# Three rounded products for the experts' down projection, on one Trainium2 core

## What is computed

```python
N_EXPERTS = 64; TOP_K = 8; D_MODEL = 1024; EXPERT_FF = 256; MOE_BLOCK = 128

def swiglu(x, w_gate, w_up, w_down):
    return (jax.nn.silu(x @ w_gate) * (x @ w_up)) @ w_down

def routed_experts(h, top_i, top_w, w_gate, w_up, w_down):
    # assignments sorted by expert, each expert's rows padded to blocks of 128
    ...
    def block(args):
        tok, e = args
        return swiglu(h_pad[tok], w_gate[e], w_up[e], w_down[e])
    out = lax.map(block, (row_tok.reshape(n_blocks, MOE_BLOCK), blk_exp))
    out = out.reshape(n_rows, D) * row_w[:, None]
    return jax.ops.segment_sum(out, row_tok, num_segments=T + 1)[:T]
```

## Time and profile before

| | us |
|---|---|
| median of 3 runs | 2048.01 |
| lowest and highest | 2043.39, 2048.45 |
| the profiled execution | 2049.21 |
| its span, first to last instruction | 2047.6 |
| mean granted TensorE clock | 0.975 of full |

### The profile page before, as it was taken

How to read it: one execution, slowest core, us unless ns; L and a number is a source line. 1 busy time by engine, 2 the same in 40 slices (tenths; PEclk the granted TensorE clock), 3 DMA queues, 4 the chain that set the end, 5 groups by cost and what they waited for, 6 DMA issues and landing times. The chain is left out here.

```text
span 2047.6 us, 34503 instructions
## 1 busy us (share of the span) xinstructions
PE 1928.1 (94%) x10264; PEld 1495.0 (73%) x10265; DVE 1038.1 (51%) x1532; ACT 874.1 (43%) x1210; POOL 373.5 (18%) x337
## 2 busy tenths in 40 slices
PE   4999999899899999989789999999999999999995
PEld 3999999899788666755547777777777777777772
DVE  4113401166438335545426666666666666666665
ACT  5110111244212212221246666666666666666663
POOL 0100100111111000000212222232223222222220
PEclk9999999899899999999889999999999999999997
DMA  7211311111443665425069896999998888897964
GB/s 260 74 52 41 123 52 31 32 63 62 144 142 113 229 230 206 143 85 196 1 228 347 261 346 182 317 295 300 331 301 271 269 273 306 244 352 253 300 180 172
DMA packets 182101, 399.64 MB, mean 195 GB/s; under 512 B 22425, under 2 KB 87185, under 8 KB 182046
## 3 DMA queue, kind: packets, MB, share of 16 engines
q1 hardware_dynamic: 149166, 312.16, 42.5%
q0 software_dynamic: 31680, 82.49, 15.7%
q10 hardware_dynamic: 1200, 4.26, 0.6%
HBM read 351.27 MB, written 80.64 MB: 211 GB/s over the span
## 5 line engine op out<-in xcount | busy, mean ns | idle before, releaser
L2184 DVE TENSOR_TENSOR wexp_lo<-wexp,wexp_hi 128x2048 fp32r<-128x2048 f32 x190 | 426.9, 2288 | 91.3 <-ACT wexp_hi L2135 88.3
L2135 ACT ACTIVATE wexp_hi<-wexp 128x2048 fp32r x190 | 353.4, 1907 | 52.4 <-issue 49.4
L2111 PE MATMUL bank<-wexp_down,hTe 128*128 x736 | 330.6, 592 | 0.0
L2086 PE MATMUL bank<-wexp_hi,x_hi 128*128 128x512 f32 x744 | 300.5, 404 | 3.8 <-DVE wexp_lo L2184 3.8
L2086 PE MATMUL bank<-wexp_hi,x_lo 128*128 128x512 f32 x744 | 292.0, 393 | 0.0
L2086 PE MATMUL bank<-wexp_lo,x_hi 128*128 128x512 f32 x744 | 290.4, 390 | 0.0
L2059 POOL DMA_INDIRECT acc_d<-ob,ixs x92 | 153.7, 1670 | 615.8 <-DMA acc_d<-ob,ixs 441.9
L2111 PEld LDWEIGHTS bank<-wexp_down,hTe 128*128 128x128 f32 x736 | 139.1, 189 | 139.4 <-issue 132.3
L547 PE MATMUL bank<-hT_hi,w_hi 128*128 128x344 f32 x576 | 187.3, 325 | 7.3 <-DVEq L659 7.3
L547 PE MATMUL bank<-hT_hi,w_lo 128*128 128x344 f32 x576 | 185.1, 321 | 0.0
L547 PE MATMUL bank<-hT_lo,w_hi 128*128 128x344 f32 x576 | 184.6, 320 | 0.0
(11 more groups left out here) (357 smaller groups left out, 2988.7 us busy)
## 6 DMA issues: line engine op xcount, KB each, us to landing
wexp<-in_w_exp_gate SPq DMA_DIRECT2D x128, 512.0 KB
wexp<-in_w_exp_up SPq DMA_DIRECT2D x128, 512.0 KB
wexp_down<-in_w_exp_down SPq DMA_DIRECT2D x128, 512.0 KB
wada<-in_w_ada SPq DMA_DIRECT2D x12, 2048.0 KB, 10.9
w_raw<-in_w_in SPq DMA_DIRECT2D x44, 512.0 KB, 3.9
gates_d<-gst POOLq DMA_DIRECT2D x48, 172.0 KB, 2.1
gate<-gates_d SPq DMA_DIRECT2D x16, 516.0 KB, 5.8
xn<-in_x_prompt ACTq DMA_DIRECT2D x8, 512.0 KB, 8.3
```

The lines of the kernel that those rows point to most:

```text
L2086: last = pe.matmul(banks[0][:].rearrange("p (g n) -> p g n", g=2), stat[:, b, k, :], mov[:, b, :, k * FF:(k + 1) * FF], start=(k == 0 and ...
L2111: last = pe.matmul(banks[4 + half][:], hT[:, f, :], wdn[:, bass.ds(slot, 1), f, half * 512:half * 512 + 512].rearrange("p a n -> p (a n)") ...
L2135: act.activation(w_hi[:, b, g, :], wexp[:, bass.ds(e & (RING - 1), 1), g, :].rearrange("p a n -> p (a n)"), ACT.Copy).then_inc(whi_ok, 1)
L2184: dve.tensor_tensor(w_lo[:, b, g, :], wexp[:, bass.ds(e & (RING - 1), 1), g, :].rearrange("p a n -> p (a n)"), w_hi[:, b, g, :], ALU.subtr ...
```

## The change

The down weights are split like the others. ACT rounds each half (`round_down`, `down_hi`), between its two `wexp_hi`; DVE takes the rest (`rest_of_down`, `down_lo`), after the first of its two `wexp_lo`; the second `wexp_lo` moves to the start of the next block, behind a table load of its own. The hidden rows are split in the same way (`turned`: `hTe_hi` by ACT, `hTe_lo` by DVE). PE takes 12 rounded products of 512 columns for the 4 in float32, and transposes the hidden rows of the next block at the end of a block, no longer at its start. The ring of the down weights has 2 slots, no longer 4, and a slot is loaded anew once it has been split. On ACT, `ob` comes after all of the splitting; `hh` takes the place of `sg`. The diff, cut to its core:

```diff
--- before.py
+++ after.py
@@ -455,7 +455,7 @@
             def far(name, shape, dt=F32):
                 return sb(name, shape, dt, c5, "right")
 
-            wdn = far("wexp_down", [P, RING, FF // P, D])
+            wdn = far("wexp_down", [P, 2, FF // P, D])
             wexp = far("wexp", [P, RING, 2, KD * FF])
             table = far("table", [1, ITEMS + AHEAD, 2], I32)
             starts = far("starts", [1, E], I32)
@@ -1909,15 +1909,18 @@
         w_lo = tile("wexp_lo", [P, 2, 2, KD * FF], F32R)
...
         sg = tile("sg", [P, FF])
-        hh = tile("hh", [P, FF])
-        hT = tile("hTe", [P, FF // P, P])
+        hh = sg
+        hT_hi = tile("hTe_hi", [P, FF // P, P], F32R)
+        hT_lo = tile("hTe_lo", [P, FF // P, P], F32R)
+        d_hi = tile("down_hi", [P, 2, FF // P, 512], F32R)
+        d_lo = tile("down_lo", [P, 2, FF // P, 512], F32R)
         ob = tile("ob", [P, 2, D])
         wcol = tile("wcol", [P, RING])
         none = tile("none", [ROW0, D // 4])
         ixs = [tile(f"ixs{b}", [P, 1], U32) for b in range(2)]
-        names = "ix ixs tp xhi xlo wc whi wlo gu sg h hp hT dn ob scat wu wd pad".split()
-        (ix_ok, ixs_ok, x_tp, xhi_ok, xlo_ok, wc_ok, whi_ok, wlo_ok, gu_ps, sg_ok, h_ok, h_tp, hT_ok, dn_ps, ob_ok, added,
-         up_ok, _, pad_ok) = (sem("s6" + n) for n in names)
+        names = "ix ixs tp xhi xlo wc whi wlo gu sg h hp hThi hTlo dhi dlo0 dlo1 dn ob scat wu pad".split()
+        (ix_ok, ixs_ok, x_tp, xhi_ok, xlo_ok, wc_ok, whi_ok, wlo_ok, gu_ps, sg_ok, h_ok, h_tp, hThi_ok, hTlo_ok, dhi_ok,
+         dlo0_ok, dlo1_ok, dn_ps, ob_ok, added, up_ok, pad_ok) = (sem("s6" + n) for n in names)
         passed = sem("s6passed")
         kept_in, ended = sem("s6kept"), sem("s6ended")
 
@@ -1945,6 +1948,10 @@
+        def down_half(e, half):
+            return wdn[:, bass.ds(e & 1, 1), :, 512 * half:512 * half + 512].rearrange("p a f n -> p (a f) n")
@@ -1968,25 +1975,23 @@
 
                 def next_down(part, g):
 
-                    at, slot = part * EG + g, g % RING
-                    before = blocks_to(at - 3)
+                    at = part * EG + g
+                    before = blocks_to(at - 1)
                     sp.wait_ge(down_in, 32 * at)
-                    sp.wait_ge(dn_ps, before)
-                    load_down(sp, a, wdn, expert_at(part, g), slot, down_in)
+                    sp.wait_ge(dlo1_ok, before)
+                    load_down(sp, a, wdn, expert_at(part, g), g % 2, down_in)
 
                 landed_up(0, 0)
                 landed_up(1, 0)
                 for e in range(2, RING):
                     load_up(sp, a, wexp, expert_at(0, e), e, up_in[e])
-                    sp.wait_ge(down_in, 32 * e)
-                    load_down(sp, a, wdn, expert_at(0, e), e, down_in)
                 for e in range(2, RING):
                     landed_up(e, 0)
                 for j in range(RING, EG):
                     next_up(0, j)
                     if j > RING:
                         landed_up(j - 1 - RING, 1)
-                next_down(0, RING)
+                        next_down(0, j - 3)
                 with sp.Fori(1, GRP) as part:
                     for g in range(EG):
                         next_up(part, g)
...
@@ -2088,34 +2093,37 @@
                                              stop=(k == KD - 1 and n == 2))
                     last.then_inc(gu_ps, 1)
 
+                def turn_hidden(j):
+                    pe.wait_ge(h_ok, j + 1)
+                    for f in range(FF // P):
+                        last = pe.transpose(banks[3][:, f * P:(f + 1) * P], hh[:].rearrange("p (n f) -> p f n", f=FF // P)[:, f, :], ident[:])
+                    last.then_inc(h_tp, 1)
+
                 pe.sem_inc(ob_ok, 2)
                 turn(0, 0, 16)
                 turn(1, 1, 16)
                 up(0, 0)
+                turn_hidden(0)
 
                 def block_of(i, q):
                     b = q % 2
-                    e = entry(pe, i, 1, E - 1)
-                    pe.wait_ge(h_ok, i + 1)
-                    for f in range(FF // P):
-                        last = pe.transpose(banks[3][:, f * P:(f + 1) * P], hh[:].rearrange("p (n f) -> p f n", f=FF // P)[:, f, :], ident[:])
-                    last.then_inc(h_tp, 1)
                     turn(i + 2, (q + 2) % RING, gathered(i, q, 2))
                     up(i + 1, 1 - b)
-                    slot = e & (RING - 1)
-                    pe.wait_ge(hT_ok, i + 1)
+                    pe.wait_ge(hTlo_ok, i + 1)
                     pe.wait_ge(ob_ok, 2 * i + 2)
-                    pe.wait_ge(down_in, e * 32 + 32)
                     for half in range(2):
+                        pe.wait_ge(dlo1_ok if half else dlo0_ok, i + 1)
                         for f in range(FF // P):
-                            last = pe.matmul(banks[4 + half][:], hT[:, f, :],
-                                             wdn[:, bass.ds(slot, 1), f, half * 512:half * 512 + 512].rearrange("p a n -> p (a n)"),
-                                             start=(f == 0), stop=(f == FF // P - 1))
-                    last.then_inc(dn_ps, 1)
+                            for n, (stat, mov) in enumerate(((hT_hi, d_hi), (hT_hi, d_lo), (hT_lo, d_hi))):
+                                last = pe.matmul(banks[4 + half][:], stat[:, f, :], mov[:, half, f, :],
+                                                 start=(f == 0 and n == 0), stop=(f == FF // P - 1 and n == 2))
+                        last.then_inc(dn_ps, 1)
+                    turn_hidden(i + 1)
 
                 blocks(pe, block_of)
                 n = blocks_done(pe)
-                pe.wait_ge(wlo_ok, n * 2 + 6)
+                pe.wait_ge(wlo_ok, n * 2 + 5)
+                pe.wait_ge(hTlo_ok, n + 1)
                 pe.wait_ge(ob_ok, n * 2 + 2)
                 pe.wait_ge(kept_in, 16 * (TILES + 3))
                 last.tensor(pe)
@@ -2128,17 +2136,31 @@
                         act.activation(x_hi[:, b, 4 * half:4 * half + 4, :].rearrange("p k n -> p (k n)"),
                                        banks[1 + half][:], ACT.Copy).then_inc(xhi_ok, 1)
 
-                def round_weights(j, b):
+                def round_weights(j, b, amid=None):
                     e = entry(act, j, 1, E - 1)
                     act.wait_ge(up_ok, e + 1)
                     for g in range(2):
+                        if g and amid:
+                            amid()
                         act.activation(w_hi[:, b, g, :],
                                        wexp[:, bass.ds(e & (RING - 1), 1), g, :].rearrange("p a n -> p (a n)"),
                                        ACT.Copy).then_inc(whi_ok, 1)
 
+                def round_down(e, j):
+                    act.wait_ge(down_in, e * 32 + 32)
+                    for half in range(2):
+                        if j is not 0:
+                            act.wait_ge(dn_ps, 2 * j - 1 + half)
+                        act.sem_inc(passed, 1)
+                        act.activation(d_hi[:, half], down_half(e, half), ACT.Copy).then_inc(dhi_ok, 1)
+
                 def gate(j):
                     act.wait_ge(gu_ps, j + 1)
                     act.activation(sg[:], banks[0][:, 0:FF], ACT.Silu).then_inc(sg_ok, 1)
+
+                def turned(j):
+                    act.wait_ge(h_tp, j + 1)
+                    act.activation(hT_hi[:].rearrange("p f n -> p (f n)"), banks[3][:, 0:FF], ACT.Copy).then_inc(hThi_ok, 1)
 
                 take(0, 0)
                 round_weights(0, 0)
@@ -2146,18 +2168,19 @@
                 round_weights(1, 1)
                 gate(0)
                 round_weights(2, 0)
+                round_down(entry(act, 0, 1, E - 1), 0)
+                turned(0)
 
                 def block_of(i, q):
                     b = q % 2
-                    act.wait_ge(h_tp, i + 1)
-                    act.activation(hT[:].rearrange("p f n -> p (f n)"), banks[3][:, 0:FF], ACT.Copy).then_inc(hT_ok, 1)
                     take(i + 2, b)
                     gate(i + 1)
-                    round_weights(i + 3, 1 - b)
-                    act.wait_ge(dn_ps, i + 1)
+                    round_weights(i + 3, 1 - b, lambda: round_down(entry(act, i + 1, 1, E - 1), i + 1))
+                    turned(i + 1)
                     act.wait_ge(wc_ok, i + 1)
                     act.wait_ge(ixs_ok, i + 1)
                     for half in range(2):
+                        act.wait_ge(dn_ps, 2 * i + half + 1)
                         act.activation(ob[:, b, 512 * half:512 * half + 512], banks[4 + half][:], ACT.Copy,
                                        scale=wcol[:, q:q + 1]).then_inc(ob_ok, 1)
 
@@ -2178,12 +2201,22 @@
                     dve.sem_inc(passed, 1)
                     dve.tensor_copy(wcol[:, q:q + 1], xg[:, q, bass.ds(e + D, 1)]).then_inc(wc_ok, 1)
 
-                def rest_of_weights(e, j, b):
-                    for g in range(2):
-                        dve.wait_ge(whi_ok, 2 * j + g + 1)
```

(42 more changed lines are left out.)

## The result

The kernel after the change takes 2124.93 us (median of 4 runs, 2121.22 to 2132.95), the kernel before, on the same chip, 2047.78: a ratio of 1.0381, interval 1.0355 to 1.0407. It is slower by 77 us, where +16 was forecast and 2120 was the upper end. The profiled execution has a span of 2119.9 us, 72.3 more than before.

The account below looks back on a forecast made before the run. PE, busy 94% of the span, was taken to bind the kernel. Loop -7, late down weights +18, start and end +5 gave +16: 2064 us for the median, range 2005 to 2120.

Parts of the forecast that it names:

- the work: In each block, PE's 12 rounded down products take 2.75 us for 3.43; ACT gains two `down_hi`, DVE two `down_lo` and `hTe_lo`.
- the three engines' sums: In the expert loop, PE, ACT and DVE each come to between 9.0 and 9.4 us a turn; none forbids a gain.
- The fewer register steps on PE cost nothing, as its queue runs ahead.: On PE, the change in register steps was to add no time.
- the 10.4: Loop turn in us above which, outside stretches with late copies, the prediction is wrong: table loads aren't hidden anywhere.
- Behind a wait they start only when it ends: On DVE, table loads behind the wait for ACT's `hTe_hi` are exposed: two loads 2.04 us, register steps 0.22.
- the ring: Waits through ACT, DVE and PE over two turns: 19.7 us, so 9.87 a turn; the loop gains 14 us.
- the forecast's first rival: Faster: DVE's two table loads hide or cost less, copies in time, PE and ACT bind; 2001 us, chance 0.25.
- the weights: ACT waits for late down copies, with two slots for four: nine waits of 2 us, 18 us.
- The scatter chain: POOL's scatter waits for the one before to land: half of the loop's 14 us gain lost, leaving -7.
- The rivals: Four other outcomes: faster (0.25), no change (0.15), slower by much by the weights (0.12) or by DVE's table loads (0.05).
- No change: Scatter chain holds the turn at 10.02 us, copies in time: +5 or less, 2045 to 2054 us; chance 0.15.
- Start and end: Before the first block and behind the last, ACT's `down_hi` and `hTe_hi` delay others: 2.5 us each, 5 in all.

Follow-up runs that it names:

- e13: e11 with, from the third expert on, the right half of the down weights' columns not copied in: 1999.94 us, ratio 0.9763 to the kernel before.
- e1: The changed kernel with PE's transposes of `hh` back at the start of its block: 2081.89 us, ratio 1.0171 to the kernel before.
- e3: The changed kernel with DVE's moved `wexp_lo` ahead of the end of the loop's body: 2085.04 us, ratio 1.0189 to the kernel before.
- e4: The changed kernel with both edits, those of e1 and e3: 2047.85 us, ratio 1.0001 to the kernel before.
- e5: The changed kernel with one more table load on PE behind the transposes of `hh`, its value unused: 2201.61 us, ratio 1.0754 to the kernel before.
- e9: e4 with four `ixs` buffers and the wait for the scatter-add's landing on ACT ahead of `ob`: 2051.22 us, ratio 1.0027 to the kernel before.
- e11: e9 with the accumulator as two 512-column tensors and two scatter-adds a block, each behind its own `ob` half and predecessor: 2045.34 us, ratio 0.9988.
- e14: e9 with, from the third expert on, the right half of the down weights' columns not copied in: 2023.67 us, ratio 0.9875 to the kernel before.
- e7_load_ahead: e4 with ACT's `ob` ahead of `hTe_hi` and DVE's table load for `wcol` ahead of its wait for `sg`: 2105.38 us, ratio 1.0291.

## Why the prediction was wrong

- **Right: the work.** 12 rounded down products in 2.73 us (2.75 forecast), `down_hi` 1.04 us, `down_lo` 1.22; and that the three engines' sums don't forbid a gain: e13 turns at 9.32 from 1100 to 1400 us.
- **Failed: "The fewer register steps on PE cost nothing, as its queue runs ahead."** It ran ahead while it met no wait that held it near the end of a block. The change put the wait for `hh` there, and the loop's own steps (tests, branches and one or two table loads, the more where the loop over four blocks and the one around it end) came to stand behind it. The transposes' old place gives 43 us back (e1), and 37 where DVE's part is mended too (e3 to e4); e5 adds one load in the new place and pays 77. This term was 0 in the sum and is 76 us in PE's phases, with some 25 more that are nearly all stretches at the lower clock. It came to 10.77 us a turn, over the 10.4 that the forecast named as a sign that it is wrong. The same mechanism I had named for DVE ("Behind a wait they start only when it ends") and not carried over to PE, whose moved wait I had priced at the 0.22 us of its transposes.
- **Mis-sized: the ring.** It was to give 9.87 us a turn, 14 us under before. The mechanism is there: DVE stands idle for table loads ahead of the `wexp_lo` that opens a block, and PE waits for `hh` about every second block. Rows of DVE (waits in the loop, then its timeline):

```profile
DVE wexp_lo L2206 <- issue: 82.2, 91, 3.1
...
1522.46 0.42 DVE L2218 TENSOR_TENSOR hTe_lo<-bank,hTe_hi 128x256 fp32r<-128x256 f32 x1
1523.68 2.29 DVE L2206 TENSOR_TENSOR wexp_lo<-wexp,wexp_hi 128x2048 fp32r<-128x2048 f32 x1 [0.80 <-issue]
```

 The two loads leave 0.90 us idle in the mean, not 2.26 with their register steps. In this turn the wait for `hTe_hi` was met early: the first load, of 0.37 us, started at 1521.88 beside `down_lo`, and only the second, 0.30 us with its steps, is in the gap. The 1.02 us of the earlier trace rows are such a load of 0.31 us and 0.6 of steps; the median of DVE's loads before is 0.31 us, half of the 600 ns that the forecast's first rival took as a floor. But DVE's own queue brings `hTe_lo` to its end at 1522.88, 8.1 us behind PE's products (1514.76), where the forecast began its count at 6.95. In this turn the part of ACT and DVE so comes to 12.8 us for 13.1, by two errors against each other. Yet e1, with PE's steps hidden, still turns at 9.29 + 92/90 = 10.3, half a microsecond above the forecast's 9.87; which member of the ring that is, the runs don't show. That the second `wexp_lo`, with its load, belongs to it, e3 shows.
- **Wrong place: the weights.** 18 us were put down for late down copies; in after ACT waits 3.8 us for them, since its turn is longer than the stream's. The moment the turn is shortened the term appears: 26 to 32 us of waits in e9 and e4, 70 in e11, and half of the bytes give e11 45 us back (e13). The forecast had the pace (12.1 us between copies of one-block experts) and forgot that a slower PE hides it. So no run shows the 18 us as a term of this change.
- **The scatter chain, 7 us,** took nothing that shows in after (DVE waits 2.9 us for landings). In the repaired kernels it stands beside the late copies; with these gone it is worth 24 us (e14 against e13). The "near 5 us" for each of POOL's waits was a wrong reading: 441.9 us in 66 are 6.7 each, and in after 311.8 in 51, 6.1.
- **The rivals.** None of the four was this. "No change" is where e4 came out, but with the copies late (31.6 us), which that rival had in time; its number there is in part luck.
- **Start and end**, 5 us in the forecast, are some 4: the first down product comes 1.8 us later, and from the last block's to the end it is 2.0 more.

Whether e11's landing chain or its late copies hold each single turn isn't told apart further; e13 took bytes from both. No run that does all the work is faster than before by more than 0.1% (e11).

## What to carry to other kernels

Before a wait is moved to the end of a loop body, list what the sequencer of that engine has to do behind it: branches, table loads and register steps are free only while the queue is ahead, and a wait that is met late takes the whole lead away. Read it in the waits by "issue" of the first instruction of a block. Here three engines and the DMA engines came to within some 10% of the turn, and 0.68 us less on PE bought nothing, even with both steps mended (e4), until a part of the transfers was left out (e13): price the transfers that a shorter turn needs.

## What the runs showed of the hardware

**A scatter instruction on POOL stretches beside a DVE subtraction with two inputs in SBUF.** Mean length in the loop, by whether it starts inside such a subtraction:

```
                scatter outside      inside            gather outside    inside
before          1.58 us (74 times)   2.06 (16)
after           1.58 (48)            2.83 (41)         1.05 (30)         2.41 (59)
e7_load_ahead   1.58 (18)            3.51 (73)
```

Outside, none is longer than 1.6 us. The Trainium skill (SBUF — State Buffer, Who interferes with whom) says that a DVE instruction with two SBUF inputs contends with a GpSimd instruction that reads SBUF; these numbers agree. The forecast had no term for it, though the change gives DVE two more such subtractions in each block; what it costs the turn, no run shows. The Trainium skill infers in the same place that a `tensor_tensor` doesn't hold up the making of descriptors; for these indirect transfers the instruction as a whole is held up, and the trace doesn't tell its reading of the list from its making of descriptors.

**A table load is short, but its tail is long:** in the loop of after PE's 94 have a median of 0.31 us and a longest of 1.32, DVE's 347 a median of 0.31 and a longest of 1.32; with its steps, exposed and with the clock it costs, one came to 0.83 a block in e5. **And idle time cost clock:** after 3.40 us of idle the granted clock fell to 1.2 GHz and the eight transposes took 1.89 us, and the mean granted clock of the whole span fell from 0.975 to 0.966 in after and 0.949 in e5, which has the longest gaps; in e4, without the gaps, it is 0.972.
